# Expert outputs added in DRAM by the scatters: one row per token instead of one per token and choice

## The chip, the cores and the metric

One core of a Trainium2 chip runs the whole program. The metric is the device time of one execution in microseconds. TensorE multiplies, VectorE and ScalarE work on SBUF and PSUM, GpSimd also issues the DMAs whose addresses come from a table (gathers and scatters), and SyncE issues all other DMAs. All DMAs of the core run on the same 16 DMA engines.

## The reference

Two transformer blocks on 512 tokens of width 1024, in float32. The change is in the last part of the second block, a mixture of 32 experts in 4 groups of 8. Each token takes one group and two experts inside it, and adds their weighted outputs to its residual; a final rmsnorm follows.

```python
g_p, g_idx = lax.top_k(jax.nn.softmax(g_logits, axis=-1), 1)
e_top, e_idx = lax.top_k(e_logits, TOP_K_IN_GROUP)          # 2 of 8 in the token's group
gate = g_p * jax.nn.softmax(e_top, axis=-1)
expert_ids = (g_idx * EXPERTS_PER_GROUP + e_idx)
...
def expert_block(args):
    xb, e = args
    return (jax.nn.silu(xb @ w_gate[e]) * (xb @ w_up[e])) @ w_down[e]
...
out = jnp.zeros((T + 1, D), y_rows.dtype).at[row_token].add(y_rows)[:T]
...
x = x + hier_moe(h2, ...)
return rmsnorm_2(x, norm_f_g)
```

## The kernel before

Up to about 1040 us the kernel does dense products (attention, MLP, linear attention, pooling, projections); their weights are streamed by SyncE in chunks. Then comes the routing on VectorE and TensorE, and then the expert stage, which the change is about.

The expert stage works in 17 units (`UNITS_E`), q = 0 to 16. A unit takes two experts, 64 rows for each (`ROWS`), on 128 partitions; unit 8 (`EXTRA_AT`) takes the rows of one expert that has more than 64 tokens. `places_of(q)` gives the places of a unit in the list of weights, `expert_at(n)` the expert at place n.

VectorE makes the tables after TensorE has counted: `list_rows` (L1576) reads ids from PSUM and writes `tabi[:, 1, :]`, the row of `x_rows` of each place, and `tabi[:, 0, :]`, its slot in `y2_rows`, which is the token's number for its first choice and 512 more for its second. Empty places get a number past the bound (`SKIP`), and the DMA leaves these out. GpSimd waits for `rows_ready` and issues four gathers ahead (`gather`, L645).

For each unit TensorE turns the gathered rows (`turn_rows`), multiplies them with gate and up weights (`gate_up`, L2146, its last products at L2152), turns the hidden rows and multiplies with the down weights (`down`, L2169). VectorE writes `ye = y * gate + xe` (`y_out`, L1630): half of the residual rides along with each of a token's two choices. GpSimd then scatters `ye` into `y2_rows` (`scatter`, L649) and issues the gather of unit q + 4. There are two `ye` buffers, so VectorE waits, before it writes `ye` of unit q, for scatter q - 2.

SyncE loads gate, up and down weights, 1 MiB each for an expert, into 6 gate and up buffers and 8 down buffers. It waits for `gate_up_done` and `down_done` of the unit that held the buffer, in the order written out in its block (L579 to L597).

The last unit (q = 16) isn't scattered. Its rows are placed by products with one-hot matrices (`hot`, L2273) in eight PSUM banks (`tail_bank(i, n)`, token block i of 128, half n of the columns). SyncE waits for all scatters and reads `y2_rows` in four pieces, one for each token block, both choices (L614). For blocks 0 and 1 VectorE adds the two choices (L1740) and then the bank (L1747). For blocks 2 and 3 TensorE adds one or both choices to the bank by products with the identity (L2279). ScalarE takes squares (L1079, of block 3 from the banks at L1083 and L1086), VectorE refines the root (L1104 to L1107) and scales (L1749, for block 3 L1756), and SyncE stores the four blocks (L618).

Of the kernel before, what the change touches and what calls it, by code (L numbers as in the profile page):

```python
# [13 lines left out]
P = 128  # L14
L = 512
# [45 lines left out]
def expert_at(n):  # L61

    return n if n < 2 * EXTRA_AT else None if n == 2 * EXTRA_AT else n - 1
# [155 lines left out]
def gated_blocks(nc, A, out):  # L219
# [8 lines left out]
    with stack:  # L228
# [127 lines left out]
        y2 = place("y2", [P, NT, 2, D], top + 2 * half_buf)  # L356
# [12 lines left out]
        y2_rows = nc.dram_tensor("y2_rows", [2 * L, D], F32).ap()  # L369
# [51 lines left out]
        def _(sp):  # L421
# [59 lines left out]
            for q in range(QUARTERS):  # L481
# [16 lines left out]
                for n in range(2 * q, 2 * q + 2):  # L498
                    sp.dma_start(y2_rows[n * P:(n + 1) * P, :], zeros[:, :]).then_inc(S("y_zeroed"), 16)
# [113 lines left out]
            for i in range(NT):  # L613
                sp.dma_start(y2[:, i, :, :], y2_rows.rearrange("(k t p) n -> t p k n", k=2, p=P)[i])\  # L614
                  .then_inc(S(f"y2_in{i}"), 16)
            for i in range(NT):
                sp.wait_ge(S("final_out"), i + 1)
                sp.dma_start(out[i * P:(i + 1) * P, :], y2[:, i, 1, :]).then_inc(S("stored"), 16)  # L618
# [4 lines left out]
        def _(pool):  # L623
# [16 lines left out]
            row_bound, slot_bound = pool.to_reg(L - 1), pool.to_reg(2 * L - 1)  # L640
# [14 lines left out]
            pool.wait_ge(S("slots_ready"), 1)  # L655
            pool.wait_ge(S("y_zeroed"), 16 * 2 * NT)
# [12 lines left out]
            def overflow(i):  # L669

                pool.wait_ge(S("over_free"), i)
                nc.gpsimd.tensor_copy(over_at[:, 1:2], tabi[:, 1, bass.ds(i + PAIRS, 1)]).then_inc(S("over_rows_set"), 1)
                pool.wait_ge(S("slots_ready"), 1)
                pool.wait_ge(S("over_rows_set"), i)
                gather((LAST_E - 1) % X_BUFS, over_at[:, 1:2], S("over_gathered"))
                pool.wait_ge(S("over_y_made"), i)
                nc.gpsimd.tensor_copy(over_at[:, 0:1], tabi[:, 0, bass.ds(i + PAIRS, 1)]).then_inc(S("over_slots_set"), 1)
                pool.wait_ge(S("slots_ready"), 1)
                pool.wait_ge(S("over_slots_set"), i)
                scatter(1, over_at[:, 0:1], S("over_scattered"))  # L680
# [40 lines left out]
        def _(act):  # L721
# [355 lines left out]
            for n in range(NT - 1):  # L1077
                act.wait_ge(S("final_sum"), n + 1)
                chain(a(xe[:, n % X_BUFS, :], y2[:, n, 0, :], ACT.Square, accum_out=gw[:, 12, n:n + 1]))  # L1079
                guess(gw[:, 12, n:n + 1], 10 + n, gw[:, 13, n:n + 1], D, gw[:, 14, n:n + 1], False)  # L1080
            one_ = slice(NT - 1, NT)
            act.wait_ge(S("block_sums"), 3)
            chain(a(xe[:, NT - 1, 0:L], tail_bank(NT - 1, 0)[:, :], ACT.Square, accum_out=gw[:, 10, one_]))  # L1083
            chain(a(gw[:, 3, one_], gw[:, 10, one_], ACT.Identity, scale=1.0 / D, bias=eps_t[:, :]))
            act.wait_ge(S("block_sums"), 4)
# [6 lines left out]
        def _(dve):  # L1092
# [274 lines left out]
            dve.wait_ge(S("y_zeroed"), 16 * 2 * NT)  # L1367
# [131 lines left out]
            chain(v.memset(tabi[:, :, :], SKIP))  # L1499
            for c in range(C_IN2 + 25, C_IN2 + 33):  # L1500
# [75 lines left out]
            def list_rows(table, rows, cols, n, rows_made, slots_made):  # L1576
# [11 lines left out]
            slot, back = list_rows(bank[1][:, 0:PAIRS], ALL_ROWS, FIRST, PAIRS, S("rows_ready"), S("slots_ready"))  # L1588
# [8 lines left out]
            token = gw[:, 8, 0:1]  # L1597
            chain(v.tensor_tensor(token, slot[:, PAIRS - 1:PAIRS], back[:, PAIRS - 1:PAIRS], ALU.add))
            for i in range(NT):
                chain(v.tensor_scalar(gw[:, 9, i:i + 1], token, -float(i * P), None, ALU.add))  # L1600
# [68 lines left out]
            def list_overflow():  # L1669
# [3 lines left out]
                list_rows(table[:, 0:OVER], LOW_ROWS, EXTRA, OVER, None, None)  # L1673
# [62 lines left out]
            for i in range(NT):  # L1736
                if i < NT - 1:
                    dve.wait_ge(S(f"y2_in{i}"), 16)
                    if i < 2:
                        chain(v.tensor_tensor(y2[:, i, 0, :], y2[:, i, 0, :], y2[:, i, 1, :], ALU.add))  # L1740
                    for n in range(2):
                        t = y2[:, i, 0, n * L:(n + 1) * L]
                        if i < 2:
                            dve.wait_ge(S("last_rows"), 2 * i + n + 1)
                        else:
                            dve.wait_ge(S("block_sums"), n + 1)
                        chain(v.tensor_tensor(t, t, tail_bank(i, n)[:, :], ALU.add), S("final_sum") if n else None)  # L1747
                if i >= 1:
                    chain(v.scalar_tensor_tensor(y2[:, i - 1, 1, :], y2[:, i - 1, 0, :], root(i - 1), gfin[:, :],  # L1749
# [570 lines left out]
```

## Time and profile before

| | |
|---|---|
| median of 3 runs | 1308.89 us (1308.36 to 1309.65) |
| profiled execution: span from first to last instruction | 1307.5 us |
| its own time beside the span | not given apart; the median is 1.4 us above the span |
| TensorE busy | 1264.9 us, 97% |
| VectorE, ScalarE, GpSimd busy | 605.1, 460.4, 532.0 us |
| DMA | 214.26 MB, mean 164 GB/s |
| read by SyncE before the end (`y<-y_rows`) | 4 DMAs of 1024 KB |

The page gives busy time, the span in 40 slices, the DMA queues and the chain that ended last. The names in rows drop buffer numbers, so `y2` and `y2_rows` stand there as `y` and `y_rows`. A busy engine isn't always a bound one: for each stage one asks who waits, and for whom. Where TensorE waits and no engine is named ("issue"), it can be a DMA. The queue q1 is that of SyncE, q0 that of GpSimd's gathers and scatters.

### The profile page before, as it was taken

To read this page: it belongs to the slowest core of one execution; us is meant where nothing else is said; L and a number is where in the kernel's file an instruction comes from. 1 tells how busy PE (TensorE), PEld (TensorE's weight loads), DVE (VectorE), ACT (ScalarE), POOL (GpSimd) and SP (SyncE) were. 2 spreads that over 40 slices of the span, in tenths; PEclk is the share of its full clock that TensorE was granted. 3 is DMA by queue.
4 is the path that set the end of the run, shared out by engine and by line. 5 is a ranking of instruction groups with operands and counts; after the bars stand their busy time and mean duration, and the time that the engine had idled before them with its cause. 6 is when DMAs were issued, how large, how long until landed. Compare 5 with 4: busy or idle time off the path is not lost.

```text
span 1307.5 us, 17452 instructions
## 1 busy us (share of the span) xinstructions
PE 1264.9 (97%) x6158; PEld 940.9 (72%) x6158; DVE 605.1 (46%) x1126; ACT 460.4 (35%) x770; POOL 532.0 (41%) x681
## 2 busy tenths in 40 slices
PE   8999999999999999999999999999999988999887
PEld 7767777788888888888888788777888863333333
DVE  4868768625442422222226765757152362222215
ACT  5557543435444333133244524165222201010102
POOL 4644323235555645545455665335554111111100
PEclk9999999999999999999999999999999999999999
DMA  7422212112334433434333333312429979999996
GB/s 225 102 65 65 66 49 65 50 54 76 112 96 113 128 97 93 133 98 129 98 95 114 89 105 81 81 48 66 129 64 349 357 271 409 424 425 424 424 425 260
DMA packets 211576, 214.26 MB, mean 164 GB/s; under 512 B 31499, under 2 KB 193021, under 8 KB 199348
## 3 DMA queue, kind: packets, MB, share of 16 engines
q1 hardware_dynamic: 202960, 203.40, 45.8%
q0 software_dynamic: 4752, 8.10, 1.7%
q10 hardware_dynamic: 3796, 1.86, 0.5%
q8 instruction: 42, 0.69, 0.2%
q14 instruction: 26, 0.21, 0.0%
HBM read 205.76 MB, written 16.78 MB: 170 GB/s over the span
## 4 chain that ended last, share of the span: by engine, by line
issue 38%; POOL 31%; PE 26%; DMA 1%; ACT 1%; DVE 1%; POOLq 0%; SPq 0%; DVEq 0%; ACTq 0%
POOL wlo L628 31%; PE bank L2152 8%; PE bank L2169 4%; PE bank L1787 3%; PE bank L1789 3%; PE bank L1788 3%; PE side L1817 1%; ACT hid L1050 1%; DMA y<-y_rows 1%; DVE hid L1620 1%; PE bank L2191 1%; PE bank L1828 1%; PE side L1789 1%; PE side L1788 1%; PE side L1787 1%
## 5 line engine op out<-in xcount | busy, mean ns | idle before, releaser
L628 POOL TENSOR_TENSOR wlo<-raw,whi 128x256 fp32r<-128x256 f32 x644 | 498.3, 805 | 523.5 <-ACT whi L732 523.3
L1788 PE MATMUL bank<-actB_lo,whi 128*128 128x512 f32 x608 | 236.7, 389 | 0.0
L1787 PE MATMUL bank<-actB_hi,whi 128*128 128x512 f32 x576 | 227.6, 395 | 0.5 <-POOL wlo L628 0.5
L1789 PE MATMUL bank<-actB_hi,wlo 128*128 128x512 f32 x576 | 224.4, 390 | 0.0
L732 ACT ACTIVATE whi<-raw 128x1024 fp32r<-128x1024 f32 x161 | 169.0, 1051 | 151.8 <-PE bank L1789 124.9
L1787 PE MATMUL bank<-actA_hi,whi 128*128 128x512 f32 x400 | 157.3, 393 | 0.6 <-DVE actA_lo L1141 0.6
L1789 PE MATMUL bank<-actA_hi,wlo 128*128 128x512 f32 x400 | 156.2, 390 | 0.0
L1788 PE MATMUL bank<-actA_lo,whi 128*128 128x512 f32 x400 | 156.2, 390 | 0.0
L1788 PEld LDWEIGHTS bank<-actB_lo,whi 128*128 128x128 f32 x608 | 114.2, 188 | 24.0 <-issue 1.0
L1787 PEld LDWEIGHTS bank<-actB_hi,whi 128*128 128x128 f32 x576 | 108.2, 188 | 25.8 <-issue 2.3
L1789 PEld LDWEIGHTS bank<-actB_hi,wlo 128*128 128x128 f32 x576 | 108.1, 188 | 22.7
L2152 PE MATMUL bank<-gu,xeT 128*64 128x512 f32 x464 | 106.8, 593 | 2.5 <-issue 2.5
L1810 PE MATMUL bank<-actA_hi,whi 128*128 128x512 f32 x216 | 95.0, 440 | 0.0
L650 POOL DMA_INDIRECT y_rows<-ye,tabi x16 | 16.1, 1004 | 187.0 <-DVE ye L1630 187.0
L1787 PEld LDWEIGHTS bank<-actA_hi,whi 128*128 128x128 f32 x400 | 75.5, 189 | 17.7 <-DVE actA_lo L1141 1.8
L2152 PEld LDWEIGHTS bank<-gu,xeT 128*64 128x64 f32 x464 | 40.6, 137 | 65.5 <-issue 65.5
L1788 PEld LDWEIGHTS bank<-actA_lo,whi 128*128 128x128 f32 x400 | 75.5, 189 | 15.6 <-issue 0.2
L1789 PEld LDWEIGHTS bank<-actA_hi,wlo 128*128 128x128 f32 x400 | 75.4, 188 | 15.7
L1812 PE MATMUL bank<-actA_hi,wlo 128*128 128x512 f32 x216 | 85.0, 394 | 0.0
L1811 PE MATMUL bank<-actA_lo,whi 128*128 128x512 f32 x216 | 84.5, 391 | 0.0
L1336 DVE TENSOR_SCALAR relu_u<-bank 128x512 f32<-128x512 f32 x32 | 22.1, 692 | 128.7 <-PE bank L1789 128.7
L1050 ACT ACTIVATE hid<-bank,slotv 128x256 f32<-128x256 f32 x17 | 12.6, 743 | 192.3 <-PE bank L2152 165.0
(401 smaller groups left out, 1668.4 us busy)
## 6 DMA issues: line engine op xcount, KB each, us to landing
dn<-in_w_exp_down SPq DMA_DIRECT2D x33, 1024.0 KB, 17.7
gu<-in_w_exp_gate SPq DMA_DIRECT2D x31, 1024.0 KB, 16.8
gu<-in_w_exp_up SPq DMA_DIRECT2D x31, 1024.0 KB, 19.7
raw<-in_w_in SPq DMA_DIRECT2D x57, 512.0 KB, 3.9
raw<-in_w_up SPq DMA_DIRECT2D x32, 512.0 KB, 3.9
raw<-in_w_down SPq DMA_DIRECT2D x32, 512.0 KB, 3.8
raw<-in_w_out SPq DMA_DIRECT2D x16, 512.0 KB, 3.9
raw<-in_w_in SPq DMA_DIRECT2D x16, 256.0 KB, 3.1
```

Source lines behind the costliest of these rows:

```text
L628: ins = nc.gpsimd.tensor_tensor(wlo[:, slot, at], raw[:, slot, at], whi[:, slot, at].bitcast(F32), ALU.subtract)
L732: a(whi[:, c % RING, :], raw[:, c % RING, :], ACT.Copy).then_inc(hi_made, 1)
L1050: a(hid[:, j, :].rearrange("s (j q) -> s q j", j=2), bank[j][:, 0:DE].rearrange("s (q j) -> s q j", j=2), ACT.Silu, scale=slotv[:, 0, p:p ...
L1336: chain(v.tensor_scalar(relu_u[:, m % 2, :], out_bank(up + m)[:, :], 0.0, None, ALU.max), chunk_freed)
L1787: mm(b[:, :], w_hi, hi[:, k, :], start=first, stop=False)
L1788: mm(b[:, :], w_hi, lo[:, k, :], start=False, stop=False)
L1789: ins = mm(b[:, :], w_lo, hi[:, k, :], start=False, stop=last)
L1810: mm(b[:, :], w_hi, actA_hi[:, k, :], start=k == 0, stop=False)
L1811: mm(b[:, :], w_hi, actA_lo[:, k, :], start=False, stop=False)
L1812: ins = mm(b[:, :], w_lo, actA_hi[:, k, :], start=False, stop=k == NK - 1)
L2152: ins = mm(bank[j][ROWS * h:ROWS * (h + 1), :].rearrange("s (g n) -> s g n", g=2), xeT[:, j, k, ROWS * h:ROWS * (h + 1)], w[:, :, k, :], s ...
L2169: ins = mm(bank[2 + n][ROWS * h:ROWS * (h + 1), :], hidT[:, j, k * P + ROWS * h:k * P + ROWS * (h + 1)], w[:, k, n * L:(n + 1) * L], start ...
```

## The change

`y2_rows` with 1024 rows becomes `y_rows` with 512, one per token. The scatters add to it (`compute_op=ALU.add`). So that no two rows of one scatter are the same token's, a unit now takes experts e and e + 16, which are in different groups. So that no two scatters are under way at once, each waits for the one before. The slots fall away, and the rows of the gather's table serve for the scatter. Four zero stores remain of eight, the final read is 0.5 MiB per block, VectorE's add of two choices falls away, and TensorE adds y by a product for block 3 alone.

```diff
 def expert_at(n):
-    return n if n < 2 * EXTRA_AT else None if n == 2 * EXTRA_AT else n - 1
+    if n == 2 * EXTRA_AT:
+        return None
+    n -= n > 2 * EXTRA_AT
+    return n // 2 + PAIRS * (n % 2)
...
-                for n in range(2 * q, 2 * q + 2):
-                    sp.dma_start(y2_rows[n * P:(n + 1) * P, :], zeros[:, :]).then_inc(S("y_zeroed"), 16)
+                sp.dma_start(y_rows[q * P:(q + 1) * P, :], zeros[:, :]).then_inc(S("y_zeroed"), 16)
...
-                sp.dma_start(y2[:, i, :, :], y2_rows.rearrange("(k t p) n -> t p k n", k=2, p=P)[i])\
-                  .then_inc(S(f"y2_in{i}"), 16)
+                sp.dma_start(y_in[:, i, 0, :], y_rows[i * P:(i + 1) * P, :]).then_inc(S(f"y_in{i}"), 16)
...
-            def scatter(n, slots, done):
-                pool.indirect_dma_start(y2_rows, bass.IndirectOffsetOnAxis(ap=slots, axis=0), ye[:, n, :], None,
-                                        bounds_check=slot_bound, oob_is_err=False).then_inc(done, 16)
+            def scatter(n, rows, done):
+                pool.indirect_dma_start(y_rows, bass.IndirectOffsetOnAxis(ap=rows, axis=0), ye[:, n, :], None,
+                                        bounds_check=row_bound, oob_is_err=False, compute_op=ALU.add).then_inc(done, 16)
...
                 pool.wait_ge(S("y_made"), q + 1)
-                scatter(q % 2, tabi[:, 0, column(q):column(q) + 1], S(f"scattered{q % 2}"))
+                if q:
+                    pool.wait_ge(S(f"scattered{(q - 1) % 2}"), 16 * ((q - 1) // 2 + 1))
+                scatter(q % 2, tabi[:, 1, column(q):column(q) + 1], S(f"scattered{q % 2}"))
...
+            chain(v.tensor_copy(const("row_id")[:, NT:2 * NT], const("row_id")[:, 0:NT]))
...
-                skip, back, slot = (prod[rows, 0, w * n:(w + 1) * n] for w in range(3))
+                skip, row = (prod[rows, 0, w * n:(w + 1) * n] for w in range(2))
                 chain(v.tensor_scalar(skip, table, 0.0, float(SKIP), ALU.is_equal, ALU.mult))
-                chain(v.tensor_scalar(back, table, float(L + 1), -float(L), ALU.is_ge, ALU.mult))
-                chain(v.scalar_tensor_tensor(slot, table, -1.0, skip, ALU.add, ALU.add))
-                chain(v.tensor_tensor(tabi[rows, 1, cols], slot, back, ALU.add), rows_made)
-                chain(v.tensor_copy(tabi[rows, 0, cols], slot), slots_made)
-                return slot, back
+                chain(v.scalar_tensor_tensor(tabi[rows, 1, cols], table, -1.0, skip, ALU.add, ALU.add), rows_made)
+                chain(v.scalar_tensor_tensor(row, table, -1.0, skip, ALU.add, ALU.add))
+                return row
...
-                    dve.wait_ge(S(f"y2_in{i}"), 16)
-                    if i < 2:
-                        chain(v.tensor_tensor(y2[:, i, 0, :], y2[:, i, 0, :], y2[:, i, 1, :], ALU.add))
+                    dve.wait_ge(S(f"y_in{i}"), 16)
...
-                    mm(tail_bank(i, n)[:, :], hot[:, i, :], ye[:, LAST_E % 2, n * L:(n + 1) * L], start=True, stop=i < 2)\
+                    mm(tail_bank(i, n)[:, :], hot[:, i, :], ye[:, LAST_E % 2, n * L:(n + 1) * L], start=True, stop=i < NT - 1)\
                         .then_inc(S("last_rows"), 1)
-                if i >= 2:
-                    pe.wait_ge(S(f"y2_in{i}"), 16)
-                    for n in range(2):
-                        for k in ((1,), (1, 0))[i - 2]:
-                            ins = mm(tail_bank(i, n)[:, :], ident, y2[:, i, k, n * L:(n + 1) * L], start=False, stop=(i, k) != (3, 1))
-                        ins.then_inc(S("block_sums"), 1)
+            pe.wait_ge(S(f"y_in{NT - 1}"), 16)
+            for n in range(2):
+                mm(tail_bank(NT - 1, n)[:, :], ident, y_in[:, NT - 1, 0, n * L:(n + 1) * L], start=False, stop=True)\
+                    .then_inc(S("block_sums"), 1)
```

VectorE after the table of ids is full (`bank` holds the ids, `prod` is scratch, `tabi` the table that gathers read), before:

```order
L1579 TENSOR_SCALAR prod<-bank 128x16 [waits table_full,dve_step]
L1580 TENSOR_SCALAR prod<-bank 128x16 [waits dve_step]
L1581 SCALAR_TENSOR_TENSOR prod<-bank,prod 128x16 [waits dve_step]
L1582 TENSOR_TENSOR tabi<-prod 128x16 [waits dve_step]
L1583 CAST tabi<-prod 128x16 [waits rows_ready]
```

The same place of the changed kernel:

```order
L1580 TENSOR_SCALAR prod<-bank 128x16 [waits table_full,dve_step]
L1581 SCALAR_TENSOR_TENSOR tabi<-bank,prod 128x16 [waits dve_step]
L1582 SCALAR_TENSOR_TENSOR prod<-bank,prod 128x16 [waits rows_ready]
L1590 COPY vals<-con 128x4 [waits dve_step]
L1591 TENSOR_SCALAR vals<-gw 128x4 [waits dve_step]
```

The table is written by the second instruction instead of the fourth.

GpSimd at the scatters of units 0 to 2 (`y_made` is VectorE's, `scattered0` and `scattered1` are landings of scatters), before and then changed:

```order
L650 DMA y_rows<-ye,tabi 1024x1024 [waits y_made,y_zeroed,slots_ready]
L646 DMA xe<-x_rows,tabi 128x1024
L650 DMA y_rows<-ye,tabi 1024x1024 [waits y_made]
L646 DMA xe<-x_rows,tabi 128x1024
L650 DMA y_rows<-ye,tabi 1024x1024 [waits y_made]
```

```order
L651 DMA y_rows<-ye,tabi 512x1024 [waits y_made,y_zeroed]
L647 DMA xe<-x_rows,tabi 128x1024
L651 DMA y_rows<-ye,tabi 512x1024 [waits scattered0,y_made]
L647 DMA xe<-x_rows,tabi 128x1024
L651 DMA y_rows<-ye,tabi 512x1024 [waits scattered1,y_made]
```

Each scatter from the second on has a wait for the landing of the one before, and the next gather stands behind it.

VectorE in the tail, from the last unit's `ye` to block 2 (`side` and `bank` are the PSUM banks with the last unit's rows), before:

```order
L1725 SCALAR_TENSOR_TENSOR ye<-bank,slotv,xe 128x512 [waits last_down_done]
L1740 TENSOR_TENSOR y_177<-y_177 128x1024 [waits y2_in0,gain_in]
L1747 TENSOR_TENSOR y_177<-y_177,side 128x512 [waits last_rows,dve_step] x2
L1740 TENSOR_TENSOR y_177<-y_177 128x1024 [waits y2_in1,final_sum]
L1747 TENSOR_TENSOR y_177<-y_177,side 128x512 [waits last_rows,dve_step] x2
L1104 TENSOR_SCALAR gw<-gw 128x1 [waits guess_made,final_sum]
L1105 TENSOR_TENSOR gw<-gw 128x1 [waits dve_step]
L1106 TENSOR_TENSOR gw<-gw 128x1 [waits dve_step]
L1107 SCALAR_TENSOR_TENSOR gw<-gw 128x1 [waits dve_step]
L1749 SCALAR_TENSOR_TENSOR y_177<-y_177,gw,gfin 128x1024 [waits dve_step]
L1747 TENSOR_TENSOR y_177<-y_177,bank 128x512 [waits block_sums,y2_in2,final_out]
L1747 TENSOR_TENSOR y_177<-y_177,bank 128x512 [waits block_sums,dve_step]
```

The changed kernel:

```order
L1739 TENSOR_TENSOR y_in<-y_in,side 128x512 [waits last_rows,y_in0,gain_in]
L1739 TENSOR_TENSOR y_in<-y_in,side 128x512 [waits last_rows,dve_step]
L1739 TENSOR_TENSOR y_in<-y_in,side 128x512 [waits last_rows,y_in1,final_sum]
L1739 TENSOR_TENSOR y_in<-y_in,side 128x512 [waits last_rows,dve_step]
L1104 TENSOR_SCALAR gw<-gw 128x1 [waits guess_made,final_sum]
L1105 TENSOR_TENSOR gw<-gw 128x1 [waits dve_step]
L1106 TENSOR_TENSOR gw<-gw 128x1 [waits dve_step]
L1107 SCALAR_TENSOR_TENSOR gw<-gw 128x1 [waits dve_step]
L1741 SCALAR_TENSOR_TENSOR y_in<-y_in,gw,gfin 128x1024 [waits dve_step]
L1739 TENSOR_TENSOR y_in<-y_in,bank 128x512 [waits last_rows,y_in2,final_out]
L1739 TENSOR_TENSOR y_in<-y_in,bank 128x512 [waits last_rows,dve_step]
```

The two adds of 1024 columns are gone, and no add waits for `block_sums`, that is for TensorE's products of y, before block 3.

## Rows read from the trace of the kernel before

**Rows 1.** The page: span, busy time, DMA share in 40 slices.
```profile
span 1307.5 us, 17452 instructions
...
PE 1264.9 (97%) x6158; PEld 940.9 (72%) x6158; DVE 605.1 (46%) x1126; ACT 460.4 (35%) x770; POOL 532.0 (41%) x681
...
DMA  7422212112334433434333333312429979999996
```

**Rows 2.** Windows: stretch, busy us of each engine, granted clock, DMA share, GB/s.
```profile
1077.00:1262.00 185.00, 166.76 (x780) 70.56 (x778) 44.55 (x70) 15.77 (x28) 27.34 (x27) 1.00 1.01 422
...
1260.00:1283.00 23.00, 19.67 (x125) 10.75 (x124) 5.26 (x9) 1.85 (x3) 1.95 (x2) 1.00 0.88 370
```

**Rows 3.** Timeline of TensorE: start, us, line, in brackets the idle time before.
```profile
1219.25 7.07 PE L2152 MATMUL bank<-gu,xeT 128*64 128x512 f32 x32
...
1232.41 7.07 PE L2152 MATMUL bank<-gu,xeT 128*64 128x512 f32 x32
...
1246.88 7.09 PE L2152 MATMUL bank<-gu,xeT 128*64 128x512 f32 x32 [1.09 <-issue]
...
1261.80 0.65 PE L2152 MATMUL bank<-gu,xeT 128*64 128x512 f32 x2 [1.44 <-issue]
```

**Rows 4.** Timeline of all engines, 1276 to 1304 us.
```profile
1276.91 0.97 POOL L650 DMA_INDIRECT y_rows<-ye,tabi  x1 [13.84 <-DVE ye L1630]
...
1282.43 2.21 SPq L614 DMA_DIRECT2D y<-y_rows  x4
...
1283.96 3.65 PE L2264 MATMUL bank<-dn,hidT 128*64 128x512 f32 x16 [0.68 <-ACT hidT L1053]
...
1287.55 3.76 PE L2273 MATMUL side<-ye,hot 128*128 128x512 f32 x8
1287.66 0.75 DVE L1725 SCALAR_TENSOR_TENSOR ye<-bank,slotv,xe 128x512 f32<-128x512 f32 x1 [0.90 <-PE bank L2264]
1288.33 1.21 DVE L1740 TENSOR_TENSOR y<-y 128x1024 f32<-128x1024 f32 x1
...
1297.18 3.60 PE L2279 MATMUL bank<-y,con 128*128 128x512 f32 x8
...
1298.02 1.28 DVE L1749 SCALAR_TENSOR_TENSOR y<-y,gw,gfin 128x1024 f32<-128x1024 f32 x1
...
1300.11 1.28 DVE L1749 SCALAR_TENSOR_TENSOR y<-y,gw,gfin 128x1024 f32<-128x1024 f32 x1
1300.87 0.60 ACT L1086 ACTIVATE xe<-bank 128x512 f32<-128x512 f32 x1 [0.70 <-PE bank L2279]
...
1302.99 1.54 DVE L1756 SCALAR_TENSOR_TENSOR y<-bank,gw,gfin 128x512 f32<-128x512 f32 x2
```

**Rows 5.** The chain that ended last, 1040 to 1062 us.
```profile
1050.84 0.18 DVE prod L1579
...
1051.46 0.19 DVE tabi L1582
...
1052.55 3.79 DMA xe<-x_rows,tabi
```

**Rows 6.** The page: the software DMA queue (packets, MB, share of 16 engines).
```profile
q0 software_dynamic: 4752, 8.10, 1.7%
```

**Rows 7.** Timeline of GpSimd.
```profile
1262.09 0.99 POOL L650 DMA_INDIRECT y_rows<-ye,tabi  x1 [13.56 <-DVE ye L1630]
```

**Rows 8.** DMA, 1262 to 1272 us: the software queue.
```profile
q0 software_dynamic: 144, 0.27, 7.0%
```

**Rows 9.** DMA, 1277 to 1283 us: 40 slices of 0.15 us, and the software queue.
```profile
GB/s 492 382 437 382 382 382 382 382 382 382 437 328 546 300 464 273 328 328 246 382 164 246 55 164 28 137 0 82 0 55 0 0 27 0 0 0 0 0 0 0
...
q0 software_dynamic: 144, 0.17, 7.9%
```

**Rows 10.** DMA, 1077 to 1262 us: the software queue.
```profile
q0 software_dynamic: 3888, 6.67, 9.4%
```

**Rows 11.** The scatter's line L650: issue to landing, least, median, most.
```profile
DMA to landing us min/median/max: 5.4/7.7/8.6
```

More of the change, by code:

```diff
@@ L354, in gated_blocks @@
             ("vals", [P, 2 * NT, 3]), ("pos", [P, 2 * NT]), ("pos_q", [P, 2 * NT]), ("over_v", [P, 4]))
-        y2 = place("y2", [P, NT, 2, D], top + 2 * half_buf)
+        y_in = place("y_in", [P, NT, 2, D], top + 2 * half_buf)
         x_out = place("x_out", [P, 2, NT, P], base + 4 * CONST_COLS["cos"][0])
@@ L368, in gated_blocks @@
         x_rows = nc.dram_tensor("x_rows", [L, D], F32).ap()
-        y2_rows = nc.dram_tensor("y2_rows", [2 * L, D], F32).ap()
+        y_rows = nc.dram_tensor("y_rows", [L, D], F32).ap()
         def x_rows_of(m):
@@ L613, in _ @@
             for i in range(NT):
-                sp.dma_start(y2[:, i, :, :], y2_rows.rearrange("(k t p) n -> t p k n", k=2, p=P)[i])\
-                  .then_inc(S(f"y2_in{i}"), 16)
+                sp.dma_start(y_in[:, i, 0, :], y_rows[i * P:(i + 1) * P, :]).then_inc(S(f"y_in{i}"), 16)
             for i in range(NT):
                 sp.wait_ge(S("final_out"), i + 1)
-                sp.dma_start(out[i * P:(i + 1) * P, :], y2[:, i, 1, :]).then_inc(S("stored"), 16)
+                sp.dma_start(out[i * P:(i + 1) * P, :], y_in[:, i, 1, :]).then_inc(S("stored"), 16)
             sp.wait_ge(S("stored"), 16 * NT)
@@ L636, in _ @@
                 second_part(c % RING, c + 1)
-            row_bound, slot_bound = pool.to_reg(L - 1), pool.to_reg(2 * L - 1)
+            row_bound = pool.to_reg(L - 1)
             for n in range(2):
@@ L1574, in _, with list_rows @@
             chain(v.reciprocal(gw[:, 8, :], gw[:, 7, :]))
[L1576 to L1578 removed]
+            def list_rows(table, rows, cols, n, rows_made):
+                skip, row = (prod[rows, 0, w * n:(w + 1) * n] for w in range(2))
                 chain(v.tensor_scalar(skip, table, 0.0, float(SKIP), ALU.is_equal, ALU.mult))
[L1580 to L1584 removed]
+                chain(v.scalar_tensor_tensor(tabi[rows, 1, cols], table, -1.0, skip, ALU.add, ALU.add), rows_made)
+                chain(v.scalar_tensor_tensor(row, table, -1.0, skip, ALU.add, ALU.add))
+                return row
             ALL_ROWS, LOW_ROWS, FIRST, EXTRA = slice(0, P), slice(0, ROWS), slice(0, PAIRS), slice(PAIRS, COLS)
             dve.wait_ge(S("table_full"), 1)
[L1588 removed]
+            row = list_rows(bank[1][:, 0:PAIRS], ALL_ROWS, FIRST, PAIRS, S("rows_ready"))
             by_k = vals[:, :, :].rearrange("p (k t) n -> p k t n", k=2)
@@ L1596, in _ @@
                                   vals[:, :, 1:3].unsqueeze(3).broadcast_to([P, 2 * NT, 2, NE]), ALU.mult), S("values_placed"))
-            token = gw[:, 8, 0:1]
-            chain(v.tensor_tensor(token, slot[:, PAIRS - 1:PAIRS], back[:, PAIRS - 1:PAIRS], ALU.add))
             for i in range(NT):
-                chain(v.tensor_scalar(gw[:, 9, i:i + 1], token, -float(i * P), None, ALU.add))
+                chain(v.tensor_scalar(gw[:, 9, i:i + 1], row[:, PAIRS - 1:PAIRS], -float(i * P), None, ALU.add))
             chain(v.tensor_tensor(hot[:, :, :], const("iota").unsqueeze(1).broadcast_to([P, NT, P]),
@@ L1672, in list_overflow @@
                 table = side[3][LOW_ROWS, 192:192 + 3 * OVER]
-                list_rows(table[:, 0:OVER], LOW_ROWS, EXTRA, OVER, None, None)
+                list_rows(table[:, 0:OVER], LOW_ROWS, EXTRA, OVER, None)
                 chain(v.tensor_copy(slotv[LOW_ROWS, :, EXTRA], table[:, OVER:].rearrange("p (n c) -> p n c", n=2)), S("over_listed"))
@@ L1755, in _ @@
                 cols = slice(n * L, (n + 1) * L)
-                chain(v.scalar_tensor_tensor(y2[:, NT - 1, 1, cols], tail_bank(NT - 1, n)[:, :], r3, gfin[:, cols],
+                chain(v.scalar_tensor_tensor(y_in[:, NT - 1, 1, cols], tail_bank(NT - 1, n)[:, :], r3, gfin[:, cols],
                                              ALU.mult, ALU.mult), S("final_out") if n else None)
@@ L2121, in table_of @@
                     for odd in range(2):
-                        rhs = placed[:, kt, :, :].rearrange("p n (c two) -> p two n c", two=2)[:, odd, :, :]
+                        rhs = placed[:, kt, :, :].rearrange("p n (two c) -> p two n c", two=2)[:, odd, :, :]
                         rhs = rhs[:, 0, :] if what == "ids" else rhs[:, 1:3, :]
```

28 lines of the change are left out of this document (11 added, 17 removed).

## Prediction

> **What bounds the kernel now.** I read the page's slices first, because they say which resource fills each stage. The reader is to see that the kernel has two stages: TensorE is busy for 97% of the span while the DMA digits are mostly 1 to 4, and in the last seventh the DMA digits are 9 [rows 1]. That last seventh is the expert stage. All that the change touches on the way to the end lies there, and the saving in bytes counts only where those bytes are waited for.
>
> Next the windows: from 1077 to 1262 us the DMA share is 1.01 at 422 GB/s, and from 1260 to 1283 us it falls to 0.88 because the last weights have come [rows 2]. TensorE is at its full clock there (granted 1.00, its 2.4 GHz level). So DMA is full, but does it set the end? The timeline of TensorE answers that. A unit of two experts starts its gate and up products 13.16 us after the one before (1219.25, 1232.41), and nothing is waited for; the last two of these start after 1.09 and 1.44 us in which the trace names no engine as releaser, and they are 14.5 and 14.9 us apart [rows 3]. Two experts are six 1 MiB weight loads, 6.29 MB, and at 424 GB/s these alone take 14.8 us. The unnamed waits are for weights. The DMA stream is thus slower than TensorE, TensorE lives on the lead of the weight buffers, and the lead is used up at unit 14. From there each microsecond more in the stream ahead of the last loads is a microsecond at the end.
>
> Last the tail. SyncE issues the read of `y2_rows` at 1282.43, when scatter 15 (issued 1276.91) has landed. The last unit's down products start at 1283.96, the products that place its rows at 1287.55, and VectorE's first add of the two y halves at 1288.33; the last product of y is at 1297.18 to 1300.78, ScalarE's last square starts at 1300.87, VectorE's last scaling at 1302.99 [rows 4]. So the 4 MiB read is part of what sets the end, but the last unit's own y, ready at about 1288.4, is near behind it.
>
> **The change, part by part.**
>
> Head: `list_rows` makes the row table after the second instruction instead of the fourth. The four stand 0.21 us apart on the chain, and the first gather, TensorE's first turn and the first weight loads of the freed buffers follow from it [rows 5]. That is 0.42 us earlier, carried through since DMA is idle there and then waits for TensorE. I take -0.4 us. The copy of `row_id` and half of the zero stores lie in stages in which TensorE is 99% busy: nothing. The new pairs (e, e + 16) load as many bytes in as many loads: nothing.
>
> Scatter with add: this is the unknown, since no transfer of the trace adds. How many bytes? The software queue, which gathers and scatters use, moves 8.10 MB [rows 6]; 1024 assignments gathered at 4 KB are 4.19, which leaves 3.91 for scatters. Scatter 14 is issued at 1262.09 and 15 at 1276.91 [rows 4, 7], and the queue moves 0.27 and 0.17 MB behind them [rows 8, 9]. So 3.47 MB belong to scatters 0 to 13, which run ahead of the weights on which unit 15 waits, in the full stretch. To add, the DMA engine must read the 4 KB row of `y_rows` besides the 4 KB row of `ye`. Bounds: at least nothing, if this read overlaps the others; if it costs what a copied row costs, 3.47 MB at 422 GB/s, 8.2 us. The queue's own share checks this: 9.4% of 185 us for 6.67 MB [rows 10] is 2.6 us per MB, 9.0 us for 3.47 MB. Above that stands a row which costs three times a copy, 16 to 18 us. The nearest row is the copied one, so I take 8.2 us. Its cover: the lead of the buffers. It is used up at unit 14 already, so none is left; waits of TensorE now begin near unit 11 or 12, since the lead shrinks by some 2 us a unit before and by 0.6 more now. Scatter 14 (0.6 us more) falls between the weights of unit 15 and of unit 16; the down weights of unit 16, the last in the queue, are in by about 1282 (the last slices of [rows 9] in which anything flows) and are wanted at 1283.96, so it is hidden.
>
> The Trainium skill (DMA: Bandwidth & Descriptors, Rules for kernel authors) says that an accumulate reads its destination and writes it later, so the second read exists; what it takes no row here shows. The Trainium skill (the same page, Where 436 GB/s comes from) says that the 16 ports of SBUF are what limits a transfer, at 435 GB/s. The 422 GB/s of the windows agree with that. By that rule the read of `y_rows`, which crosses no such port, would be free, the sum would be -2.7 us, and it is my first rival.
>
> New wait of a scatter for the one before: a scatter is issued every 13.2 to 14.8 us, and lands 5.4 to 8.6 us after its issue [rows 11]. 13.2 - 8.6 leaves 4.6 us, so the wait costs nothing as long as the add lengthens a landing by less. Behind it on GpSimd stands only the gather of unit q + 4, wanted three units later.
>
> Tail: the read is 2 MiB instead of 4. Today its first 1 MiB piece is in by 1288.33 at the latest, where the add of halves starts [rows 4]; half of it less is 1.2 us at 422 GB/s, so 1287.1. VectorE wants it at 1288.45 (second half of `ye`, 1287.66 + 0.75), which hides 1.3 us of a later landing of scatter 15. VectorE then has no add of halves (two of 1.21 us) and TensorE 2 products of y instead of 6. What is late next? TensorE: eight products at 0.94 us (3.76 for four) from 1287.55, then two, about 1296.5. VectorE in its order: first add 1288.45, second half when its product is done, 1290.15; token block 1 to 1292.0; refining and scaling of block 0 in 2.09 (1298.02 to 1300.11 in today's rows, of which 1.28 is the scaling), 1294.1; adds of block 2, 1295.6; then twice 2.09, 1299.8; the last sum and refining 1.0, so the last scaling starts at 1300.8 instead of 1302.99. ScalarE comes to 1300.5 by the way from its last square (1302.99 - 1300.87 = 2.12 after it). VectorE sets the end: -2.2 us, and with ScalarE's finding 2.4; I take -2.3. Of the 2 MiB saved only this is on the path, since the last unit's y is not ready sooner.
>
> Sum: -0.4 + 8.2 - 2.3 = +5.5 us on the profiled span of 1307.5. What lies around the span is the same for both, and the median, 1308.89, is 1.4 above that span: 1314.4 us.
>
> **The rivals.**
>
> The read of the destination is free (up to about a third of a copy): the SBUF side is the limit, and the stream of weights keeps 424 GB/s while rows are added. For it: gathers and weights, which both end in SBUF, mix at the same rate. Against it: nothing in the trace is limited elsewhere, so the trace can't tell. Then 1308.9 - 2.7 = 1306.2, up to 1309.0. The sign turns where the add costs 2.7 us, a third of a copy. This is the side of faster or no change.
>
> The add costs more than a copy (1.4 to 3 times): +11.5 to +24.6 - 2.7, so 1317.7 to 1331. For it: two addresses are touched in DRAM by one packet, and one waits for the other. Against: packets of several queues share an engine, so a wait can be filled.
>
> The chain of scatters becomes the bound: if a landing exceeds 13.2 us, each scatter holds the next, and the `ye` buffer of unit q + 2 with it. A landing of 15 us would give 15 x 1.8 = 27 us, less the 2.5 us now waited: 1333 or more. Against it: the landing would have to grow by 4.6 us over today's longest, for some 4 rows on each engine.
>
> That the saving in the read is worth its 5 us of bytes I give little, since unit 16's y holds the tail.
>
> **How the numbers follow.** Forecast (add costs 0.7 to 1.4 copies, 1311.9 to 1317.7): 0.42. Free read: 0.27. In between, 1309 to 1311.9: 0.06. Dearer: 0.17. Chain: 0.08. A difference of 0.2%, 2.6 us, is what a measurement can tell here, so faster is below 1306.3 and slower above 1311.5. The free read lies on that edge, and I split it 0.12 faster and 0.15 same; with the case between, same is 0.20, slower 0.68. The range from 1305.5 to 1325 leaves out some 0.05 below and 0.14 above (the chain and the dear end). The likeliest case alone is 1311.9 to 1317.7.
>
> **What would show it.** Right: in 1077 to 1262 the DMA share stays at 1.0 while GB/s of payload falls or the software queue's share rises by about 4 points; TensorE's unnamed waits before the gate products start near unit 12 and sum to some 10 us instead of 2.5; the last down products start about 7.8 us later than 1283.96; from there to the last scaling it is 16.7 us instead of 19.0; the first gather starts 0.4 us sooner. Wrong: those waits still begin at unit 14 (free read), a scatter's landing above 13 us with waits of GpSimd for `y_rows` (chain), or VectorE waiting for `y_in` in the tail (the read still on the path).

## The result and the profile after

The changed kernel takes 1316.3 us (median of 4 runs, 1314.4 to 1318.4) against 1309.3 for the kernel before: 1.0056 times as long, with a 95% interval of 1.0044 to 1.0068. It is 7.0 us slower; 5.5 were forecast.

The page of the changed kernel, with the rows that answer to [rows 1] and [rows 6]:

```profile
span 1316.2 us, 17438 instructions
...
PE 1262.0 (96%) x6150; PEld 936.7 (71%) x6150; DVE 602.0 (46%) x1120; ACT 460.4 (35%) x770; POOL 541.6 (41%) x681
...
DMA  7422212122333333334333333213329989999995
...
q0 software_dynamic: 4752, 8.18, 2.5%
```

As many packets of the software queue as before carry nearly the same payload, and take 2.5% of the engines' time instead of 1.7%. The payload doesn't count the row that an add reads; only the time does. The windows (stretch, busy us of each engine, granted clock, DMA share, GB/s), with the answer to [rows 2] first; the last one lies inside the products of unit 13, and is taken up at the end:

```profile
1077.00:1262.00 185.00, 161.17 (x738) 66.70 (x735) 41.38 (x65) 14.69 (x26) 34.76 (x27) 0.98 1.02 402
1204.00:1222.00 18.00, 14.91 (x72) 5.80 (x67) 4.59 (x7) 1.12 (x2) 2.63 (x2) 1.00 1.02 416
1222.00:1238.00 16.00, 12.26 (x58) 5.07 (x58) 2.72 (x5) 1.13 (x2) 2.63 (x2) 1.00 1.02 408
...
1240.00:1244.00 4.00, 3.10 (x8) 1.11 (x10) 0.00 (x0) 0.00 (x0) 1.37 (x2) 0.50 1.02 420
```

The DMA engines are as full as before (1.02), but move 402 GB/s of payload where they moved 422. The timeline of TensorE, first products of gate and up in units 11 to 16, answers to [rows 3]:

```profile
1206.95 7.09 PE L2144 MATMUL bank<-gu,xeT 128*64 128x512 f32 x32 [0.32 <-issue]
...
1223.62 7.09 PE L2144 MATMUL bank<-gu,xeT 128*64 128x512 f32 x32 [3.29 <-issue]
...
1240.90 9.70 PE L2144 MATMUL bank<-gu,xeT 128*64 128x512 f32 x32 [3.89 <-issue]
...
1257.41 7.09 PE L2144 MATMUL bank<-gu,xeT 128*64 128x512 f32 x32 [0.51 <-issue]
...
1272.52 7.09 PE L2144 MATMUL bank<-gu,xeT 128*64 128x512 f32 x32 [1.62 <-issue]
...
1285.71 7.11 PE L2245 MATMUL bank<-gu,xeT 128*64 128x256 f32 x64
```

With a single 1.15 us at unit 7 the unnamed waits add up to 10.8 us, where they were 2.5. They start at unit 11 instead of 14, apart from the one at unit 7. How much one row costs is read where the queue has one scatter and no gather. Two such windows of the changed kernel, 1274 to 1284 us and 1262 to 1268 us (share of 16 engines last):

```profile
q0 software_dynamic: 144, 0.23, 12.0%
```

```profile
q0 software_dynamic: 144, 0.13, 12.0%
```

The first is 10 us x 16 x 12.0% = 19.2 us of engine time for 0.23 MB, which is 56 rows of 4 KB: 343 ns a row, the empty packets included. The second is 11.5 us for 32 rows, 360 ns, with more empty packets to each row. The same sum over [rows 8] gives 11.2 us for 66 rows, 170 ns. An added row takes twice the time of a copied one. (The packets' own records have 159 ns for a copied row and 327 for an added one, both at the median.) The records don't say what fills the second half of that time, the reading of the old row or a wait for it. The tail answers to [rows 4]:

```profile
1287.64 1.55 POOL L651 DMA_INDIRECT y_rows<-ye,tabi  x1 [13.44 <-DVE ye L1627]
...
1294.69 3.65 PE L2256 MATMUL bank<-dn,hidT 128*64 128x512 f32 x16 [0.68 <-ACT hidT L1053]
1295.33 1.75 SPq L616 DMA_DIRECT2D y_in<-y_rows  x4
...
1298.27 3.76 PE L2265 MATMUL side<-ye,hot 128*128 128x512 f32 x8
...
1299.53 0.69 DVE L1739 TENSOR_TENSOR y_in<-y_in,side 128x512 f32<-128x512 f32 x1 [0.40 <-PE side L2265]
...
1305.30 1.88 PE L2269 MATMUL bank<-y_in,con 128*128 128x512 f32 x4
...
1309.35 1.28 DVE L1741 SCALAR_TENSOR_TENSOR y_in<-y_in,gw,gfin 128x1024 f32<-128x1024 f32 x1
...
1311.64 1.54 DVE L1748 SCALAR_TENSOR_TENSOR y_in<-bank,gw,gfin 128x512 f32<-128x512 f32 x2
```

From the last down products to the last scaling it is 16.95 us (1311.64 - 1294.69) instead of 19.03. Every kernel below with the short tail and the 2 MiB read has 16.95 or 16.96 here. But the last down products start 10.7 us later than before in this execution, and 7.4 us later (1291.38) in that of e0, the same kernel again; single executions differ by that much. A scatter lands 7.6 to 11.1 us after its issue, against [rows 11]:

```profile
DMA to landing us min/median/max: 7.6/9.1/11.1
```

### The profile page after: what moved, and what is told of

Read it like the earlier page. It is cut to its first block, busy times and chain, and to the rows that moved or that the text cites. A ratio compares the mean times of both kernels' runs of the same rounds, so it can differ in the third digit from the quotient of the medians.

```text
span 1316.2 us, 17438 instructions
## 1 busy us (share of the span) xinstructions
PE 1262.0 (96%) x6150; PEld 936.7 (71%) x6150; DVE 602.0 (46%) x1120; ACT 460.4 (35%) x770; POOL 541.6 (41%) x681
## 4 chain that ended last, share of the span: by engine, by line
issue 39%; POOL 31%; PE 25%; DVE 2%; ACT 2%; POOLq 0%; DMA 0%; DVEq 0%; ACTq 0%
POOL wlo L629 31%; PE bank L2144 8%; PE bank L2161 4%; PE bank L1779 3%; PE bank L1781 3%; PE bank L1780 3%; PE side L1809 1%; ACT hid L1050 1%; DVE hid L1617 1%; PE bank L2183 1%; PE side L1780 1%; PE side L1779 1%; PE side L1781 1%; PE bank L2245 1%; PE side L2067 1%
## 5 line engine op out<-in xcount | busy, mean ns | idle before, releaser
L2144 PE MATMUL bank<-gu,xeT 128*64 128x512 f32 x464 | 109.5, 606 | 10.8 <-issue 10.8
L651 POOL DMA_INDIRECT y_rows<-ye,tabi x16 | 25.4, 1585 | 189.7 <-DVE ye L1627 189.7
L1779 PEld LDWEIGHTS bank<-actA_hi,whi 128*128 128x128 f32 x400 | 75.1, 188 | 19.2 <-DVE actA_lo L1141 3.5
```

The source lines that it names most:

```text
L651: pool.indirect_dma_start(y_rows, bass.IndirectOffsetOnAxis(ap=rows, axis=0), ye[:, n, :], None, bounds_check=row_bound, oob_is_err=False, ...
L1779: mm(b[:, :], w_hi, hi[:, k, :], start=first, stop=False)
L2144: ins = mm(bank[j][ROWS * h:ROWS * (h + 1), :].rearrange("s (g n) -> s g n", g=2), xeT[:, j, k, ROWS * h:ROWS * (h + 1)], w[:, :, k, :], s ...
```

## The experiments

Each was timed in 5 rounds beside the kernel before on the same chip, e0 to e3 on one chip, e4 to e7 on a second and e8 to e10 on a third. Differences are taken between ratios, times 1309 us; between runs of different groups they lean on both chips having the same ratio.

| kernel | median us | ratio to before (95%) |
|---|---|---|
| e0 changed kernel again | 1316.55 | 1.0055 (1.0042 to 1.0069) |
| e1 new pairs alone | 1311.03 | 1.0016 (1.0007 to 1.0025) |
| e2 changed, no add | 1307.95 | 0.9989 (0.9980 to 0.9998) |
| e3 changed, halves even | 1316.16 | 1.0048 (1.0034 to 1.0062) |
| e4 changed, adds in units 0 to 7 | 1313.49 | 1.0052 (1.0038 to 1.0066) |
| e5 changed, adds in units 8 to 15 | 1309.13 | 1.0018 (1.0009 to 1.0027) |
| e6 changed, reads twice | 1319.89 | 1.0098 (1.0083 to 1.0114) |
| e7 changed, halves more uneven | 1318.33 | 1.0091 (1.0075 to 1.0106) |
| e8 e2 and e6 together | 1308.73 | 1.0002 (0.9992 to 1.0011) |
| e9 changed, every second pair crossed | 1316.76 | 1.0053 (1.0040 to 1.0067) |
| e10 before, half the read | 1308.30 | 1.0002 (0.9993 to 1.0011) |

The kernel before had a median of 1309.3 beside e0 to e3, 1307.0 beside e4 to e7 and 1309.0 beside e8 to e10, so the medians of e4 to e7 lie lower; the ratios are what can be compared. e2, e4, e5 and e8 leave out additions of a token's two choices and e10 leaves out the second choice, so they serve for timing alone.

**Where the gain and the loss come from.** The changed kernel once more:

> The changed kernel once more, beside the three that follow. Measured so far: ratio 1.0056 to the kernel before. Every theory expects 1.005 to 1.006 (about 1316).

It repeated, at +7.2 us. Without the add:

```diff
-                                        bounds_check=row_bound, oob_is_err=False, compute_op=ALU.add).then_inc(done, 16)
+                                        bounds_check=row_bound, oob_is_err=False).then_inc(done, 16)
```

> The changed kernel with plain copies in place of adds: a row of y_rows then holds the choice that was scattered last, so the sum over the two choices is left out; bytes, waits, pairs and tail stay. Theory A (an added row holds a DMA engine for 327 ns instead of 159, and the fuller half takes 67 rows an engine): 9 to 11 us faster than the changed kernel, 1306 to 1307.5. Theory B (the add costs 8.2 us as predicted, and something else 1.5): 1308. Theory C (the waits of one scatter for another cost): no gain, 1316.

The adds cost 8.6 us by the ratios (1.0055 - 0.9989), uncertain by about 2 us. That lies between what theories A and B gave, so the run doesn't part them, but it rules out C: the waits of the scatters for each other are still in this kernel. It also shows what the rest of the change is worth: 1.4 us (0.3 to 2.6).

The pairs alone, in the kernel before:

```diff
-    return n if n < 2 * EXTRA_AT else None if n == 2 * EXTRA_AT else n - 1
+    if n == 2 * EXTRA_AT:
+        return None
+    n -= n > 2 * EXTRA_AT
+    return n // 2 + PAIRS * (n % 2)
...
-                        rhs = placed[:, kt, :, :].rearrange("p n (c two) -> p two n c", two=2)[:, odd, :, :]
+                        rhs = placed[:, kt, :, :].rearrange("p n (two c) -> p two n c", two=2)[:, odd, :, :]
```

> The kernel before with one edit: a unit takes experts e and e + 16, and the tables follow; slots, plain scatters and the 4 MiB read stay. Theory A (the pairs put 540 scattered rows on partitions 64 to 127 and 430 on 0 to 63, where it was 458 and 493, and the DMA engines that serve the fuller half end later): 110 rows more on 8 engines, 13.8 each, by 2 x 159 ns (gather and scatter) is 4.4 us between the halves instead of 1.4, so 1 to 2 us slower than before. Theory B (the step of the prediction: pairs cost nothing): within 0.3 us of before.

It is 2.1 us slower by the ratio (0.9 to 3.3), 1.7 by the medians. The same weights are loaded by as many DMAs. What has changed is the place of the rows, their number (970 scattered instead of 951, since the last unit has fewer) and the order of the experts. The reference's router gives the four groups 120, 97, 186 and 109 tokens on these inputs. Experts e of groups 0 and 1 now always lie on partitions 0 to 63 and those of groups 2 and 3 on 64 to 127. Without the last unit that is 430 scattered rows below and 540 above; with even and odd experts it was 493 and 458.

The trace doesn't say which DMA engine a packet ran on. It does say how the engines stop, as the share of 16. Windows of e1 and of the kernel before, around the end of the weights:

```profile
1275.00:1279.00 4.00, 4.00 (x40) 3.19 (x38) 0.70 (x3) 0.71 (x1) 0.98 (x1) 1.00 0.71 295
```

```profile
1275.00:1279.00 4.00, 4.00 (x40) 3.23 (x38) 1.42 (x3) 0.32 (x1) 0.97 (x1) 1.00 0.98 408
```

With the new pairs part of the engines are done while the others still load (0.71 against 0.98). How much time that is worth, these two executions don't show: from the gate products of unit 1 to those of unit 16 e1 takes 200.65 us and the kernel before 200.39, and e1's tail is 19.37 us instead of 19.03, 0.6 us in all. The Trainium skill (DMA: Bandwidth & Descriptors, The descriptor swizzle) gives engines 0 to 7 the partitions 0 to 63 and the others 64 to 127, for a plain 1 MiB transfer; the rows agree with that for the indirect ones, and a row further down, with a share of exactly one half, agrees best.

**Is it the fuller half?** Three other pairings of the changed kernel, adds kept. The lines of the products that fill the two tables, which follow the pairs, are left out of the three cuts. In e3 expert 2c is below and 2c + 17 above:

```diff
-    return n // 2 + PAIRS * (n % 2)
+    return n - n % 2 if n % 2 == 0 else (n + PAIRS) % NE
...
```

> The changed kernel, adds kept, with other pairs: expert 2c in the lower half and 2c + 17 (mod 32) in the upper, also of different groups, so 493 rows below and 454 above are scattered. It costs 8 small products more for each of two tables, about 0.5 us on the way to the first gather. Theory A (fuller half): about 14 rows less on the engines that end last, at 327 + 159 ns, half of it over the mean: 2 to 4 us faster than the changed kernel, 1313. Theory B (pairs cost nothing): 1316 to 1317.

In e7 the pairs are (e, e + 8), the lower half gets groups 0 and 2:

```diff
-    return n // 2 + PAIRS * (n % 2)
+    c = n // 2
+    return 16 * (c // 8) + 8 * (n % 2) + c % 8
...
```

> The changed kernel, adds kept, with the pairs (e, e + 8) inside groups 0 and 1 and inside groups 2 and 3: 598 rows scattered from partitions 0 to 63 and 387 from 64 to 127, where it is 430 and 540. Theory A (the DMA engines of the fuller half set the end): gathers 612 x 159 ns and scatters 0 to 13, 511 x 327 ns, over 8 engines are 33.1 us, against 30.1 in the changed kernel: 3.0 us slower, 1319.3. Theory B (only the number of rows matters, not where they lie): 1316.3.

In e9 the halves of every second unit are exchanged:

```diff
-    return n // 2 + PAIRS * (n % 2)
+    c = n // 2
+    return c + PAIRS * (n % 2 ^ c % 2)
...
```

> The changed kernel, adds kept, pairs e and e + 16 kept, but the two halves of every second unit exchanged, so 491 rows below and 479 above are scattered. It costs 16 small products more in each of two tables, 1.1 us on the way to the first gather. Theory A (fuller half sets the end): gathers and adds of the fuller half take 27.8 us instead of 30.1, so -2.3 + 1.1: 0 to 2.5 us faster than the changed kernel, ratio 1.0035 to 1.0055, and the DMA share falls from 1.0 later and more steeply. Theory B (only the number of rows matters): 1.1 us slower, ratio 1.0064.

e7 is 4.7 us slower than the changed kernel by the ratios, with intervals that don't meet, though it was timed on another chip: theory B, that only the number of rows counts, doesn't fit. e3 and e9 gained 0.9 and 0.3 us by the ratios, less than the measurement can tell from nothing. Their traces show two things that work against each other: DMA ends more evenly, but the stage starts later. The windows from 1283 to 1287 us, of the changed kernel, then of e9, then of e7:

```profile
1283.00:1287.00 4.00, 4.00 (x26) 2.07 (x24) 1.05 (x2) 0.00 (x0) 0.00 (x0) 1.00 0.60 248
```

```profile
1283.00:1287.00 4.00, 4.00 (x34) 2.70 (x32) 1.42 (x3) 0.00 (x0) 1.00 (x1) 1.00 0.97 408
```

```profile
1283.00:1287.00 4.00, 4.00 (x32) 2.58 (x30) 1.42 (x3) 0.00 (x0) 0.64 (x1) 1.00 0.50 213
```

With the most uneven halves, e7, half of the engines' time is used in these 4 us, with the crossed pairs nearly all of it: in e7 it is as if eight engines loaded the last weights while eight are done.

And the products of the id table with the write of `tabi` behind them, of the changed kernel, then of e9:

```profile
1048.87 1.11 PE L2118 MATMUL bank<-placed,at_row 128*64 128x16 f32 x32
1050.35 0.17 DVE L1581 SCALAR_TENSOR_TENSOR tabi<-bank,prod 128x16 int32<-128x16 f32 x1
```

```profile
1049.14 2.06 PE L2122 MATMUL bank<-placed,at_row 128*64 128x8 f32 x64
...
1051.52 0.17 DVE L1582 SCALAR_TENSOR_TENSOR tabi<-bank,prod 128x16 int32<-128x16 f32 x1
```

The more numerous products take 0.9 us more (2.38 against 1.48), and a second table follows. Taken from the start of unit 1's gate products to that of unit 16's, which leaves the head out, the profiled executions have 212.3 and 210.6 us (changed kernel, twice), 209.9 (e3), 209.3 (e9) and 213.3 (e7). A row taken at 159 ns in a gather and 327 in an add, over 8 engines, gives the fuller half 30.1, 28.9, 27.8 and 33.1 us (my estimate; 30.1 is 565 rows gathered and 461 added). From the mean of the two the steps are -1.6 for -1.1, -2.2 for -2.3, +1.9 for +3.0. The order agrees, but these are single executions, and two of the same kernel lie 1.7 us apart, so they support the account and don't size it. e1, e3 and e7 also change the order in which the experts' weights are loaded, and no run varies that alone. That the fuller half ends last is seen in the shares; what it costs in time isn't settled. My expectation for e3, 2 to 4 us, was too high: it took the halves to come out even, while up to the last weights 541 rows are gathered and 445 added below, and 483 and 405 above.

**Early adds or late adds?** In e4 units 0 to 7 add and the others copy, in e5 the reverse. The call gets a last argument that says whether to add:

```diff
-                scatter(q % 2, tabi[:, 1, column(q):column(q) + 1], S(f"scattered{q % 2}"))
+                scatter(q % 2, tabi[:, 1, column(q):column(q) + 1], S(f"scattered{q % 2}"), q < 8)
...
```

> The changed kernel, adding in units 0 to 7 alone and copying in the others; so the sum over two choices is left out where the later scatter copies. Theory A (every added row ahead of the last weights costs 168 ns of its DMA engine, and the fuller half, partitions 64 to 127, sets the end; 317 rows there in these units): 317 x 0.168 / 8 = 6.7 us above the kernel without adds (1307.95), 1314.6. Rival D (the lead of the weight buffers hides what is added early, and only late adds cost): within 1 us of 1308.

> The changed kernel, adding in units 8 to 15 alone and copying before, the counterpart. Theory A: 144 rows of the fuller half fall in units 8 to 13, 3.0 us above 1307.95, so 1311; units 14 and 15 are hidden. Rival D (only late adds cost): the whole 8.6 us, 1316.5.

By the ratios the early adds cost 8.2 us and the late ones 3.8. The rival that the lead of the weight buffers hides early adds is refuted: in e4 the last added scatter is issued at 1167 us, and TensorE's first wait of over 2 us for weights ends at 1220, yet these adds cost most of the whole. Both expectations counted the rows of the fuller half wrongly. It has 347 in units 0 to 7 and 114 in units 8 to 13, not 317 and 144; the sum of 461 was right. By the same rate that is 7.3 and 2.4 us, against 8.2 and 3.8 measured. The two sum to 12.0 us, where all adds together cost 8.6; each of the differences is uncertain by about 2 us, so this is not in conflict, but the sizes are not known better than that.

**What the tail gained.** The changed kernel with each block read twice:

```diff
-                sp.dma_start(y_in[:, i, 0, :], y_rows[i * P:(i + 1) * P, :]).then_inc(S(f"y_in{i}"), 16)
+                for k in range(2):
+                    sp.dma_start(y_in[:, i, k, :], y_rows[i * P:(i + 1) * P, :]).then_inc(S(f"y_in{i}"), 16)
...
-                    dve.wait_ge(S(f"y_in{i}"), 16)
+                    dve.wait_ge(S(f"y_in{i}"), 32)
...
-            pe.wait_ge(S(f"y_in{NT - 1}"), 16)
+            pe.wait_ge(S(f"y_in{NT - 1}"), 32)
```

VectorE and TensorE wait for both reads of a block.

> The changed kernel, which reads each block of y_rows twice, into both halves of its buffer, so 4 MiB again as before the change; VectorE and TensorE still do only the shorter work. Theory A (the shorter chain of VectorE gave the 2.1 us of the tail, the bytes were hidden by the last unit's y): the last block lands 3 us after TensorE wants it (some 13 us after SyncE's issue), of which about 1 us shows: 1317 to 1318. Rival (the bytes were on the path): the whole 2.1 us of the tail is lost, 1318.5 or more, and VectorE waits at block 0 and 1.

e8 has this edit and that of e2, plain copies in place of adds:

> Plain copies in place of adds (the sum over two choices is left out) and 4 MiB read, with the short chain of the tail. Reading twice cost the adding kernel 3.6 us between the last down products and the last scaling (20.5 instead of 16.95). Theory T1 (an added scatter lands later, so the read starts 0.7 us after the last down products instead of 1.0 before them, and only thus is the read so long on the path): 1.7 us of the 3.6 fall away, a tail of 18.8 to 19.0 and 1.0 to 1.5 us slower than before would be with the copy kernel's 0.9989: ratio 1.000 to 1.001. Theory T2 (4 MiB cost 3.6 us wherever they start): tail 20.5, ratio 1.0015 to 1.002.

In e10 the kernel before reads the first choices alone and uses them twice:

```diff
-                sp.dma_start(y2[:, i, :, :], y2_rows.rearrange("(k t p) n -> t p k n", k=2, p=P)[i])\
-                  .then_inc(S(f"y2_in{i}"), 16)
+                sp.dma_start(y2[:, i, 0, :], y2_rows[i * P:(i + 1) * P, :]).then_inc(S(f"y2_in{i}"), 16)
...
-                        chain(v.tensor_tensor(y2[:, i, 0, :], y2[:, i, 0, :], y2[:, i, 1, :], ALU.add))
+                        chain(v.tensor_tensor(y2[:, i, 0, :], y2[:, i, 0, :], y2[:, i, 0, :], ALU.add))
...
```

> The kernel before with half the read (first choices alone, so the second choices are left out), but with all adds of VectorE and all six products of y on TensorE, fed with the same half twice. Theory T3 (TensorE's 14 products at 0.94 us set the tail as soon as the bytes don't): products end where they end now, tail 19.0, ratio 0.999 to 1.000. Rival (the bytes alone make the tail long): tail 17, ratio 0.998.

My theory for e6 fell. It is 5.6 us slower than the changed kernel by the ratios, not 1, and its tail takes 20.5 us (1293.79 to 1314.30), 3.6 more. The other 2 us are not placed; the two were timed on different chips. Its timeline:

```profile
1293.79 3.65 PE L2257 MATMUL bank<-dn,hidT 128*64 128x512 f32 x16 [0.68 <-ACT hidT L1054]
1294.46 4.71 SPq L617 DMA_DIRECT2D y_in<-y_rows  x8
...
1299.40 1.41 DVE L1740 TENSOR_TENSOR y_in<-y_in,side 128x512 f32<-128x512 f32 x2 [1.17 <-DMA y_in<-y_rows]
...
1303.44 1.41 DVE L1740 TENSOR_TENSOR y_in<-y_in,side 128x512 f32<-128x512 f32 x2 [2.63 <-DMA y_in<-y_rows]
...
1308.29 3.78 PE L2270 MATMUL bank<-y_in,con 128*128 128x512 f32 x4 [3.73 <-DMA y_in<-y_rows]
...
1314.30 1.54 DVE L1749 SCALAR_TENSOR_TENSOR y_in<-bank,gw,gfin 128x512 f32<-128x512 f32 x2
```

VectorE waits for the read at blocks 0 and 1 and TensorE at block 3, whose two products then take 3.78 us instead of 1.88, at a granted clock of 0.50. In e8 the same 4 MiB cost 0.5 us; its rows for the same places:

```profile
1281.97 4.70 SPq L617 DMA_DIRECT2D y_in<-y_rows  x8
...
1282.92 3.65 PE L2257 MATMUL bank<-dn,hidT 128*64 128x512 f32 x16 [0.68 <-ACT hidT L1054]
...
1290.17 1.41 DVE L1740 TENSOR_TENSOR y_in<-y_in,side 128x512 f32<-128x512 f32 x2 [0.83 <-DMA y_in<-y_rows]
...
1295.84 1.98 PE L2270 MATMUL bank<-y_in,con 128*128 128x512 f32 x4 [2.14 <-DMA y_in<-y_rows]
...
1300.40 1.54 DVE L1749 SCALAR_TENSOR_TENSOR y_in<-bank,gw,gfin 128x512 f32<-128x512 f32 x2
```

Its tail is 17.5 us (from 1282.92 to 1300.40). The read starts 0.95 us before the last down products there and 0.67 after them in e6, since an added scatter lands later. Theory T1 named the right mechanism, but 3.0 of the 3.6 us fell away, not 1.7. 1.8 of these 3.0 are the products of block 3, which ran at the lower clock in e6 and not in e8 (3.78 us against 1.98); the 1.2 left go with the start of the read. So the later start costs time twice: once as a longer wait, and once by what the clock does after it. The end of e10's tail:

```profile
1282.75 3.65 PE L2263 MATMUL bank<-dn,hidT 128*64 128x512 f32 x16 [0.68 <-ACT hidT L1052]
...
1301.19 1.54 DVE L1755 SCALAR_TENSOR_TENSOR y<-bank,gw,gfin 128x512 f32<-128x512 f32 x2
```

That is 18.4 us: with half the bytes and the long chain it gains 0.6, and T3 is about right (its whole time, at a ratio of 1.0002, doesn't tell so small a gain). So of 19.0 us in the kernel before, the shorter chain alone gives 1.5, fewer bytes alone 0.6, and both 2.1. In the changed kernel, where the read starts later, the fewer bytes save 3.6.

## Why the prediction was right, point by point

The forecast was 5.5 us slower with 1305.5 to 1325 as the range; 7.0 were measured. The range is wide enough to hold the 1306.2 of the first rival too, so lying in it proves little; what bears the mechanism out are e2, the 343 ns and the marks named beforehand.

- Head, -0.4: from the start of the id table's products to the write of `tabi` it is 1.48 us instead of 1.89 (1049.57 to 1051.46), so 0.41. It is too small to be seen in the times of whole runs.
- Scatter with add, +8.2: measured 8.6 (e2). The value was bounded by the nearest row, a copied one, and an added row takes just that more: 343 ns against 170. That it would cost just one more copy was a choice of the nearest row, with a chance of 0.42, and not worked out. That the cost is carried to the end, and that early adds are no cheaper, was shown by e4 and e5. Payload that falls (to 402 GB/s) at a full DMA share, a rise of the software queue's share by about 4 points (from 9.4% to 13.1%), and waits of some 10 us in all (10.8) had been named as marks of it.
- Free read, the first rival: refuted by the 343 ns and by e2. The Trainium skill (DMA: Bandwidth & Descriptors, Where 436 GB/s comes from) names the ports of SBUF as the bottleneck, at 435 GB/s; a read that crosses no such port still took the engines' time here, and the payload fell from 422 to 402 GB/s.
- The new pairs, "nothing": this step failed. As many bytes in as many loads is true, but the rows of a table column are tied to partitions, and, by the shares, the halves of the partitions to halves of the DMA engines. e1 has 2.1 us for it (0.9 to 3.3), which is the whole of what that run shows, not of the place alone: at 159 ns a row the fuller half takes 20.4 us in e1 and 19.6 in the kernel before, 0.8 us more (an estimate from the packets' records). From e2 comes a third value: it is 1.4 us faster than the kernel before where head and tail gain 2.5, which leaves 1.1 for the pairs. So the sum lacked a term of 0.8 to 2.1 us, and with it would have been 6.3 to 7.6.
- The parts, each as measured (-0.4, +8.6, +2.1, -2.1), add up to 8.2 us, 1.2 more than the 7.0 of the whole. That is within the uncertainty of 8.6 and 2.1, but neither of the two is known better than to 1 or 2 us.
- New wait, nothing: right. (The price of the chain rival leaves out the 2.7 us saved elsewhere: by its own terms 1330.7, not 1333.) GpSimd waits for VectorE's `ye` alone (189.7 us in 16 waits), and never for a landing. The longest landing, 11.1 us, left 2.1 us of the 13.2.
- Tail, -2.3: 2.1 measured. But the reason given was only half of it. I called it the work of the shorter chain, with 1.3 us of cover for a later landing; in fact the read's start moved by 2.2 us against the last down products (1.5 us before them, now 0.6 after), and without the halved read the tail would have been 3.6 us longer (e6), 1.9 of them at the lower clock.
- No version here that computes the whole result beats the kernel before. e2 shows that with adds that cost no more than copies the change would gain 1.4 us (0.3 to 2.6).

## What to carry to other kernels

A DMA that adds to DRAM cost its rows twice in engine time here, so it halves the rows to be read later at the price of the rows that it writes. It can pay only where the DMA engines have time to spare, and here they were full for 200 us before the read that it made shorter. When rows are dealt to partitions by a table, count them by half of the partitions, gathers and scatters together: here the engines of the fuller half were the last to load. And a transfer that is hidden now may be so by 1 us only; before calling its bytes free, look at what its start depends on and whether the same change moves that.

## What the runs showed of the hardware

- An indirect scatter that adds holds GpSimd's instruction for 1.59 us instead of 1.01, and lands 1.2 us later at the median when issued at the same unit pace (9.1 against 7.9 in e2, which has the same rows).
- TensorE's clock fell to its lower level (granted 0.50, 1.2 GHz) in the middle of the expert stage of the changed kernel, after a wait of 3.89 us in a stretch in which it had been busy for 12.3 of 16 us. The products of unit 13 took 9.70 us instead of 7.09. It seems to have cost nothing here: the next wait for weights was only 0.51 us, while the DMA share stayed at 1.02. That is argued from this execution; every kernel here that adds in all units shows such a fall in its profile, so none serves as the comparison. In e6's tail, where nothing covers it, block 3's products took 1.9 us longer in the same way, after a wait of 3.73 us; after one of 2.14 us in e8 they took 1.98 us, 0.1 longer.
- A share of 0.50 of the 16 engines over 4 us (e7) with uneven halves, against 0.97 (e9) with nearly even ones and 1.02 before the last weights: the engines stop in two groups of eight, as they would if the rows of the lower and of the upper 64 partitions loaded different ones.
